# Head of a hybrid decoder kernel: the norm weight spread by the matrix engine, a fourth row buffer, uneven column pieces, and three pieces of projection moved

## The reference, cut to what matters

```python
h = rmsnorm(x, w['pre_g'])          # x: 1024 + 32 rows of 1024, f32
u = h @ w['w_in']                   # 1024 x 3584
qa, ka, va, za, xb, ob, zb = jnp.split(u, SPLITS, axis=-1)
...
xc, new_buf = causal_conv(xb, conv_buf, w['conv_w'], w['conv_b'])
xch = jax.nn.silu(xc).reshape(B, S, H_B, DH_B)
qb = jnp.einsum('bshd,hde->bshe', xch, w['wq_b'])
...
(C1, n1, m1), h = lax.scan(step, carry0, ...)      # mLSTM, in chunks
```

## Time and profile before

| | |
|---|---|
| time of three runs, us | 990.39 median, 989.72 to 991.27 |
| profiled execution: its own time, us | 992.28 |
| profiled execution: span of the trace, us | 990.6 |
| PE busy, share of the span | 924.0 us, 93% |
| DVE, ACT, POOL busy | 49%, 40%, 11% |
| chain that ended last, by engine | PE 82%, DMA 5%, SP's queue 4%, DVE 4%, ACT 3% |

### The profile page before, as it was taken

How to read it: one execution, slowest core, us unless ns; L and a number is a source line. 1 busy time by engine, 2 the same in 40 slices (tenths; PEclk the granted TensorE clock), 3 DMA queues, 4 the chain that set the end, 5 groups by cost and what they waited for, 6 DMA issues and landing times.

```text
span 990.6 us, 18543 instructions
## 1 busy us (share of the span) xinstructions
PE 924.0 (93%) x6995; PEld 738.6 (75%) x6995; DVE 489.7 (49%) x1081; ACT 391.9 (40%) x840; POOL 108.6 (11%) x233
## 2 busy tenths in 40 slices
PE   4999989999999999997899999997869999999996
PEld 3989979999888888886466677765548786677774
DVE  5643845555474455453575655455464443433223
ACT  5443253333334643345444544454453222421211
POOL 2300000000000000003000023341110000000000
PEclk9989989999999999999999999999999999999998
DMA  7362215222332222224976789967984522213221
GB/s 233 89 173 65 65 48 146 65 65 65 102 107 66 84 78 73 64 65 137 358 248 220 229 267 337 348 200 225 315 282 165 191 86 69 65 20 129 75 91 43
DMA packets 115266, 142.36 MB, mean 144 GB/s; under 512 B 9623, under 2 KB 75799, under 8 KB 115178
## 3 DMA queue, kind: packets, MB, share of 16 engines
q1 hardware_dynamic: 109418, 122.31, 38.5%
q0 software_dynamic: 5760, 18.88, 5.5%
HBM read 125.34 MB, written 15.41 MB: 142 GB/s over the span
## 4 chain that ended last, share of the span: by engine, by line
PE 82%; DMA 5%; SPq 4%; DVE 4%; ACT 3%; issue 2%; POOL 1%; POOLq 0%; ACTq 0%; DVEq 0%
PE ps L1949 72%; PE ps L1952 10%; DMA Kr<-in_cache_k 2%; DMA Vr<-in_cache_v 2%; SPq L580 1%; DMA xrow<-in_x_prompt 1%; SPq L576 1%; PE ps L1944 1%; SPq L562 1%; DVE pp L1763 0%; DMA wst<-in_w_in 0%; POOL small L735 0%; ACT wh L939 0%; ACT junk L1218 0%; ACT whi L898 0%
## 5 line engine op out<-in xcount | busy, mean ns | idle before, releaser
L1949 PE MATMUL ps<-hhi,whi 128*128 128x272 f32 (+1 forms) x672 | 229.0, 341 | 1.2 <-DVE hlo L1283 1.2
L1949 PE MATMUL ps<-hhi,wlo 128*128 128x272 f32 (+1 forms) x672 | 219.2, 326 | 0.0
L1949 PE MATMUL ps<-hlo,whi 128*128 128x272 f32 (+1 forms) x672 | 218.9, 326 | 0.0
L1949 PE MATMUL ps<-wh,r 128*128 128x512 f32 (+1 forms) x544 | 155.3, 401 | 0.1
L1949 PEld LDWEIGHTS ps<-hhi,whi 128*128 128x128 f32 x672 | 129.3, 192 | 14.0 <-issue 3.7
L1949 PEld LDWEIGHTS ps<-hlo,whi 128*128 128x128 f32 x672 | 129.4, 193 | 9.9 <-issue 1.9
L1949 PEld LDWEIGHTS ps<-hhi,wlo 128*128 128x128 f32 x672 | 128.9, 192 | 9.2
L1949 PEld LDWEIGHTS ps<-wh,r 128*128 128x128 f32 (+1 forms) x544 | 99.4, 185 | 26.2 <-issue 1.0
L1299 DVE TENSOR_TENSOR wlo<-wst,whi 128x1024 fp32r<-128x1024 f32 x56 | 68.8, 1229 | 84.5 <-ACT whi L898 84.5
L1728 DVE COPY kTs<-ps 128x512 f32<-128x512 f32 x64 | 44.1, 689 | 67.3 <-PE ps L1952 67.2
L1952 PEld LDWEIGHTS ps<-ident,Kr 128*128 128x128 f32 x512 | 56.2, 141 | 26.5 <-issue 22.5
(11 more groups left out here) (355 smaller groups left out, 1333.0 us busy)
## 6 DMA issues: line engine op xcount, KB each, us to landing
Kr<-in_cache_k SPq DMA_DIRECT2D x128, 256.0 KB, 4.2
wst<-in_w_in SPq DMA_DIRECT2D x56, 512.0 KB, 3.7
Vr<-in_cache_v POOLq DMA_DIRECT2D x72, 256.0 KB, 4.8
Vr<-in_cache_v SPq DMA_DIRECT2D x56, 256.0 KB, 4.3
out_y_prompt<-rows SPq DMA_DIRECT2D x16, 512.0 KB, 2.9
xrow<-in_x_prompt SPq DMA_DIRECT2D x8, 512.0 KB, 4.7
wout<-in_w_out SPq DMA_DIRECT2D x8, 512.0 KB, 5.7
rows<-in_x_prompt SPq DMA_DIRECT2D x8, 512.0 KB, 4.3
```

The costliest lines, as they stand in the source:

```text
L1949: return nc.tensor.matmul(out, lhsT, rhs, start=start, stop=stop, **more)
```

## The change

- `gpre`: one row of 4 KB is loaded; PE multiplies a column of ones with it (two matmuls of 512 columns into banks 2 and 3), and DVE copies the 128 x 1024 result to `gpre` ahead of its first `scale_x`.
- `xrow` gets a fourth slot, and SP's order changes: x0, the gpre row, x1, w0, x2, x3, w1, x4, x5, w2, x6, then the small parameters, x7, x8. Before, the small parameters stood behind x2.
- Half 0 is cut at column 256, not 272: pieces of 256 and 288 columns. The first four pieces are w0 and w1 on the first 256 columns, then w0 and w1 on the rest (`OPENING`), so that p0 needs two row tiles, not three. Three turns, not four, stand ahead of p0, and `head_bank` gives the third turn banks of its own. w0 is in use until p2 is done, w1 until p3 (`WEIGHTS_DONE` 3, 4).
- w4 is asked for ahead of the wait for `vec_ready`, `lam_ready` and the state loads.
- Fills: one piece more in the head; two instead of one behind the turn of the parameters (`vecT`) and behind `folded` (ahead of the wait for the sample's convolution); one new ahead of the wait for `s_hn`; twelve pieces behind chunk 3 become eight. ACT and DVE follow with their own fills.
- A semaphore that nobody waited for goes.

The core of the diff:

```diff
-PIECE = FIRST // 2
+COLS = (slice(0, 2 * P), slice(2 * P, FIRST))
...
-WEIGHTS_DONE = [2 * w + 2 if w < NT else NT + w + 1 for w in range(WEIGHTS)]
+OPENING = [(0, 0), (1, 0), (0, 1), (1, 1)]
+WEIGHTS_DONE = [3, 4] + [2 * w + 2 if w < NT else NT + w + 1 for w in range(2, WEIGHTS)]
...
+def piece_at(p):
+
+    return OPENING[p] if p < len(OPENING) else divmod(p, 2)
+
+
+def head_bank(o):
+
+    return 0 if o == 2 else 4 + 2 * ((o if o < 2 else o - 1) % 2)
...
             load_x(0)
-            sp.dma_start(gpre, io["norm_pre_g"][0:1, :].broadcast_to([P, D])).then_inc(s["gpre_in"], 16)
+            sp.dma_start(gpre[0:1, :], io["norm_pre_g"][0:1, :]).then_inc(s["gpre_in"], 16)
             load_x(1)
             load_w(0)
             load_x(2)
+            load_x(3)
+            load_w(1)
+            load_x(4)
+            load_x(5)
+            load_w(2)
+            load_x(6)
...
         @block.vector
         def _(dve):
-            dve.wait_ge(s["gpre_in"], 16)
+            dve.wait_ge(*done["gpre_spread"])
+            nc.vector.tensor_copy(gpre, ps[:, 2:4, :].rearrange("p a b -> p (a b)")).then_inc(*signal["gpre_stored"])
+            dve.wait_ge(*done["gpre_stored"])
...
-            fill(3)
+            fill(4)
             dve.wait_ge(*done["weights_T"])
...
             last.then_inc(*signal["wg_stored"])
-            fill()
+            fill(2)
...
             conv_first(15, 16)
-            fill()
+            fill(2)
             dve.wait_ge(*done["s_rs"])
...
             for i in range(H):
                 chunk(i)
-            fill()
             finish(H - 1)
-            fill(3)
             dve.wait_ge(s["piece_done"], 2 * NT)
...
         def _(pe):
             pe.wait_ge(*done["ident_ready"])
+            pe.wait_ge(s["gpre_in"], 16)
+            for c in range(2):
+                last = nc.tensor.matmul(ps[:, 2 + c, :], ones[0:1, :], gpre[0:1, c * 512:(c + 1) * 512], start=True, stop=True)
+            last.then_inc(*signal["gpre_spread"])
...
             last.then_inc(*signal["folded"])
-            fill()
+            fill(2)
...
             turn(ps[0:SMP, 6, 0:DH], Cs[:, :, DH], "s_nrow")
+            fill()
             pe.wait_ge(*done["s_hn"])
...
             fill()
             finish(H - 1)
-            fill(11)
+            fill(7)
```

More of the change, by code:

```diff
@@ L444, in program @@
                 signal[name], done[name] = (steps_done, 1), (steps_done, n + 1)
-        x_in = [sem(f"x_in{n}") for n in range(3)]
+        x_in = [sem(f"x_in{n}") for n in range(4)]
         w_in = [sem(f"w_in{n}") for n in range(3)]
@@ L513, in _ @@
             sp.dma_start(bias_f, io["b_if"][0, H:2 * H].rearrange("(h o) -> h o", o=1)).then_inc(s["params_in"], 16)
[L514 to L517, removed]
+            load_x(7)
+            load_x(8)
             load_heads(0)
@@ L521, in _ @@
             load_w(3)
+            load_w(4)
             sp.wait_ge(*done["vec_ready"])
@@ L911, in evict @@
                 if e < 2 * NT:
-                    tile, c = ORDER[e // 2], e % 2
-                    nc.scalar.activation(U0[:, tile, c * PIECE:(c + 1) * PIECE], ps[:, bank_of(e), 0:PIECE], ACT.Copy
-                                         ).then_inc(s["u_stored"], 1)
+                    w, c = piece_at(e)
+                    out = U0[:, ORDER[w], COLS[c]]
+                    nc.scalar.activation(out, ps[:, bank_of(e), 0:out.shape[1]], ACT.Copy).then_inc(s["u_stored"], 1)
                 else:
@@ L939, in copy @@
                 nc.scalar.activation(out, in_, fn, **more).then_inc(*(s[name], 1) if name in s else signal[name])
-            for o in range(3):
-                square_x(o)
+            square_x(0)
+            square_x(1)
+            split(0)
+            square_x(2)
             store_hi(0)
-            split(0)
+            square_x(3)
             store_hi(1)
-            square_x(3)
             store_hi(2)
-            square_x(4)
-            store_hi(3)
-            for o in range(4, 9):
+            fill()
+            for o in range(3, 9):
                 if o < 8:
                     square_x(o + 1)
-                fill()
                 store_hi(o)
-            fill()
+                if o < 8:
+                    fill()
             act.wait_ge(s["lam_sum"], 2)
@@ L1308, in fill @@
                 filled[0] += n
-            for o in range(3):
-                scale_x(o)
+            scale_x(0)
+            scale_x(1)
+            rest(0)
+            scale_x(2)
             store_lo(0)
-            rest(0)
             store_lo(1)
@@ L1316, in _ @@
             store_lo(2)
-            scale_x(4)
-            store_lo(3)
-            for o in range(4, 9):
+            fill()
+            for o in range(3, 9):
                 if o < 8:
                     scale_x(o + 1)
-                fill()
                 store_lo(o)
+                if o < 8:
+                    fill()
             dve.wait_ge(s["params_in"], 16 * PARAMS)
@@ L1967, in piece @@
                 if p < 2 * NT:
-                    out, ks, hi, lo = ps[:, bank_of(e), 0:PIECE], range(KC), hhi[0], hlo[0]
-                    cols = slice(part * PIECE, (part + 1) * PIECE)
+                    cols = COLS[part]
+                    out, ks, hi, lo = ps[:, bank_of(e), 0:cols.stop - cols.start], range(KC), hhi[0], hlo[0]
                 else:
@@ L1986, in fill @@
                 filled[0] += n
-            for o in range(4):
+            for o in range(3):
                 turn_h(o)
[L1990 to L1996, removed]
+            for o in range(3, 9):
+                fill()
+                turn_h(o)
             fill()
@@ L2130, in chunk @@
                 for h in range(H):
-                    last = turn(ps[:, 4, h * P:(h + 1) * P], x[h])
-                last.then_inc(s["kvtok_ready"], 1)
+                    turn(ps[:, 4, h * P:(h + 1) * P], x[h])
                 if i == 0:
```

52 lines of the change are left out of this document (25 added, 27 removed).

## The result

| | before | changed |
|---|---|---|
| median of ten executions each, us | 989.62 | 998.36 |
| lowest and highest, us | 986.43, 992.50 | 994.39, 1002.15 |
| ratio of the changed kernel to before, 95% interval | | 1.0083, 1.0063 to 1.0103 |
| profiled execution, span, us | 990.6 | 998.5 |

The change makes the kernel slower by 0.83%, about 8.2 us. The prediction said 2.6 us slower, with 997.0 as the upper end; the direction held, the size and the range didn't.

The account below looks back on a forecast made before the run. PE, busy 93% of the span, bounds the kernel, so only its waits and clock count. With gains positive, 1.2 + 1.3 − 2.4 + 2.6 − 3.1 − 2.2 = −2.6 takes 990.4 to 993.0 us; range 988.0 to 997.0.

Parts of the forecast that it names:

- C: Ahead of the sample's convolution: DVE's rest of w7 makes PE wait 3.5 us; 2.4 us lost, no clock fall priced.
- more falls of the clock: Rival: one more fall at the new waits in the head, at C or ahead of chunk 0 gives 995.5 us; chance 0.2.
- E: The sample's turn: a piece covers the wait for `s_hn`, leaving 2.2 us ahead of chunk 0; 2.6 us gained.
- A: The head: p0 starts 3.8 us sooner, at 17.5, but p2 waits for row tile 4; 1.2 us gained.
- B: Up to the gate weights: the extra piece behind `vecT` covers the 1.40 us state-load wait; net 1.3 us gained.
- G: Behind chunk 3: p62 waits 3.95 us for the rest of w31; net 3.1 us lost, plus 2.2 for a clock fall.
- The second rival: The rival called more falls of the clock, at 995.5 us; chance 0.2.
- The first rival: In the head: the clock is already up at p0, which takes 3.0 us; 991.3 us in all, chance 0.2.
- Shift alike: Chunks 4 to 7 and all that follows move by the same amount, with no further gain or loss.

Follow-up runs that it names:

- run 5: Only the head of the change on the kernel before, with the rest that its extra piece pushed ahead of the sample's convolution put behind it; 988.07 us, ratio 0.9976.
- run 9: The kernel with both repairs, last two convolutions together on DVE ahead of the last rest; pieces behind chunk 3: nine 985.09, eight 986.94, ten 989.24 us.
- run 2: The changed kernel with the rest of w7 behind the sample's convolution on DVE, as before the change; 990.36 us, ratio 1.0008.
- the head alone: Only the head of the change on the kernel before, fills behind it as before, eleven pieces behind chunk 3; 993.18 us, ratio 1.0025.
- run 6: The kernel with both repairs, with the piece ahead of `s_hn` put back behind chunk 3, nine pieces there; 988.79 us, ratio 0.9979.
- the repair: The changed kernel with the rest of w31 ahead of the first convolution behind chunk 3 on DVE, each later rest one convolution sooner; 995.98 us, ratio 1.0051.
- the kernel with both repairs: The changed kernel with the rest of w31 made sooner and the rest of w7 behind the sample's convolution on DVE; 988.68 us, ratio 0.9983.

## Why the prediction was wrong

**The step that failed is the price of the clock at C**, where the sum prices a new wait of 3.5 us and no fall. The sum holds the clock once, as −2.2 behind chunk 3; without it the sum is −0.4. By the table the low clock costs the changed kernel 24.4 us and the kernel before 14.6, 9.8 more, and all the rest is 2.4 us *less*; with the uncounted 1.5 us at p0 put in its place, 8.3 more and 0.9 less. On balance the loss lies in the falls. Each new fall stands at a wait that the prediction had named, and "more falls of the clock" was a rival at 0.2 and one fall. A second term, E, was forecast as a gain of 2.6 and brought none.

The runs lead from the kernel before to the changed one a step at a time, with these differences of ratios (each good to about 3 us):

| step | us, minus is faster | forecast, same sign |
|---|---|---|
| the head, its extra rest behind the convolution (run 5) | −2.4 | A −1.2 |
| a piece behind `folded`, last rest last: ten pieces (9) | −0.1 | none |
| a piece behind `vecT`: nine pieces (9) | −3.7 | B −1.3 |
| a piece ahead of `s_hn`: eight pieces (9) | +1.7 | E −2.6 |
| DVE's old order of rests behind chunk 3 (2) | +5.2 | G and its clock +5.3 |
| the rest of w7 ahead of the convolution: the changed kernel | +7.4 | C +2.4 |

So the largest term, G, came out as priced, within that error. C is 5.0 us off, E 4.3, and A and B gave more than forecast. That the sum missed by only 5.6 us is in part luck: the errors of A and B stand against those of C and E.

The upper end was also added up wrongly. The second rival, 995.5, with the lower ends of B (1.3 less) and E (2.1 less) is 998.9, not 997.0.

- **A, the head, +1.2.** Product 3.75 (3.5 forecast), copy until 9.8 (9.6), first turn 11.15 (10.9), p0 at 17.71 (17.5), p2 at 28.30 (28.4) behind a wait of 1.75 (2.3). Mechanism and places held. What the head gives is 2.4 us by run 5, twice the term. The first rival (clock up by p0) is what most profiles show: in eight of the eleven profiles with the product p0 ran at full speed. In both of the changed kernel and in one other the clock was up by the third turn but fell again at p0, at 17.53 in the first. The prediction gave the rival 0.2 and argued against it from turns alone, without the product ahead of them.
- **B, +1.3.** A and B together are 2.5 in the timeline (54.70), as forecast. The wait at p8 was 0.17, not 0.6.
- **C, −2.4.** The wait is 3.3, and the timeline gives −2.2. But "the clock was already low behind it, so I price no fall" was wrong. One profile of the kernel before had that fall; the second didn't. A fall that a 0.8 us wait brings sometimes stands at the longer wait, 2.9 to 3.7 us, in all four profiles that have it. Undoing this edit alone was worth 7.4 us, and 4.9 in the head alone. This is the largest single error, 5 us over the term.
- **E, +2.6.** From −0.3 to −2.9 at the first `wkv` product, 2.5. But the clock fell at the 2.2 us wait for `nout` in both profiles of the changed kernel (143.8, 144.7), where I priced none. And the piece was worth as much behind chunk 3: the kernels that have it there are 0.4 us (run 6) and 1.7 us (run 9) faster by ratios, neither clear of noise. With it ahead of `s_hn`, the 3.4 us wait for `nd` is traded for 2.3 for `nout`, 0.9 for `G` and some short ones; in the two kernels of run 9 PE's waits from 20 to 310 us sum to 8.1 us with eight pieces and 6.5 with nine.
- **G, −3.1 and −2.2.** 3.5 us of wait for 3.95, and 6.8 us at 0.50 that cost the top of the forecast, 3.4, not 2.2: from −2.9 to +5.4 with what the fall behind `nout` costs. Without the repair's own new wait (run 9, eight pieces) a 0.5 us wait is left, and the place is worth 5.2 us by ratios against 5.3 in the sum.
- **After chunk 4.** "Shift alike" holds roughly. The two pairs of profiles stand 5.4 and 7.1 us apart at chunk 4 (303.92 to 298.50, and 304.56 against 297.43 below) and 7.9 and 8.0 at the end; the falls behind 460 us add and take a few us, unlike from one execution to the next.

```profile
297.43 1.05 PE L1949 MATMUL ps<-xch,wqk 128*128 128x128 f32 x8
```

**Where a fall is chance.** The kernel with both repairs and the one with eight pieces and the last rest last are the same program up to chunk 3, and in both PE waits 2.3 us for `nout`. The wait ends at 136.64 in the one and at 140.29 in the other. The windows behind it, first of the one, then of the other:

```profile
137.00:141.00 4.00, 4.00 (x44) 3.68 (x43) 0.69 (x1) 0.62 (x3) 0.00 (x0) 1.00 0.02 4
```

```profile
141.00:144.40 3.40, 3.40 (x27) 2.76 (x27) 0.69 (x1) 0.55 (x2) 0.00 (x0) 0.51 0.02 5
```

In the first the record has no fall up to 292 us. So what was forecast as yes or no is a chance with a price. The fourteen profiles give a count behind the head, up to 310 us, of the falls that begin within 2.2 us of the end of a wait:

| wait, us | for | with a fall |
|---|---|---|
| 2.9 to 3.7 | `xchS`, `nd`, rest of w31 | 11 of 11 |
| 2.6 | `nd`, chunk 4 | 6 of 7 |
| 2.3 | `nout` | 5 of 7 |
| 1.4 to 1.7 | state loads | 4 of 5 |
| 0.8 to 1.0 | `xchS` | 2 of 3 |
| 0.9 | `G` | 0 of 10 |

The longest waits had one each time. Below that the length alone doesn't tell, since waits of 0.8 to 1.0 us had one at one place and never at another, and in the kernel with nine pieces one stands behind a wait of 0.4 us. No run changes the length of one wait and nothing else, so how the chance grows with it stays open. Nor is it shown how the 7.4 us of run 2 divide between falls at the place itself and falls later on; the table gives 5.4 of them to the clock (24.4 to 19.0) and 1.4 to the rest, 0.6 being the spread of the means.

## What to carry to other kernels

Where pieces are dealt out in turn and every second one carries work for another engine, one piece more upstream turns the parity of all that follows: print the order on each engine and look at what stands ahead of each hand-over, not only at the place that was edited. Where PE is busy 93% of the time, as here, price a new wait of 3 us or more with a fall of the clock behind it: here such a wait of 3.3 us cost 7.4. A piece that is moved to cover one wait is worth only what it takes off the sum of all waits. And one profile doesn't tell whether a fall of the clock belongs to the program: average the mean clock over the executions before calling a stretch slow already.

## What the hardware showed that was not expected

The mean clock, as plain as it is, explained the result: 0.985 for the kernel before and 0.976 for the changed one, 1% of 990 us. With two f32 products from one partition ahead of the turns, the clock rose at 14.12 to 17.44 us rather than 20.83, and in the kernel with both repairs, where it rose at 15.64, the third turn took 1.10 us rather than 1.97. So a product that was put on the critical path of the head paid for part of itself with the clock. And two executions of one program, with all waits behind the head alike to 0.2 us, differed by 4.0 us in span (990.6 and 986.6), while (1 − clock) × span differs by 4.7 us between them.
